# Compression weights transferred straight into the operand buffer, and a wait per attention tile in block 1's output

## The chip, the cores and the metric

The kernel runs on 1 core of one Trainium2 chip. The metric is the device time of one execution, in microseconds; lower is better. The unchanged kernel is the comparison.

## What is computed

Two transformer blocks run one after the other on 256 tokens of width 1024, all in float32. Block 1 has depth 1, block 2 has two layers. The core of it, cut to what bears on the change:

```python
def first_block(x, mem, ...):
    for l in range(DEPTH):
        x = x + 0.5 * swiglu(rms_norm(x, ffn1_norm[l]), ffn1_w_in[l], ffn1_w_out[l])
        ...
        mixed = jnp.concatenate([y_lru, y_moba.astype(x.dtype), y_mem.astype(x.dtype)], axis=-1)
        x = x + mixed @ w_out[l]
        x = x + 0.5 * swiglu(rms_norm(x, ffn2_norm[l]), ffn2_w_in[l], ffn2_w_out[l])

def compress(t, pos_emb, w1, b1, w2):
    b, s, g, d = t.shape
    chunks = t.reshape(b, s // CMP_STRIDE, CMP_STRIDE, g, d)
    blocks = jnp.concatenate([chunks[:, :-1], chunks[:, 1:]], axis=2)
    blocks = blocks + pos_emb[None, None, :, None, :]
    flat = jnp.moveaxis(blocks, 3, 2).reshape(b, -1, g, CMP_BLOCK * d)
    return jax.nn.gelu(flat @ w1 + b1) @ w2

def token_mixer(h, mem, ...):
    ...
    k_cmp = compress(kv[:, :, 0], cmp_pos_k, ck_w1, ck_b1, ck_w2)
    v_cmp = compress(kv[:, :, 1], cmp_pos_v, cv_w1, cv_b1, cv_w2)
    ...
    y_nsa = nsa_attention(q, q_rot, k_cmp, v_cmp, k_slc, v_slc, k_win, v_win, gates)
    ...
    g_conv, g_nsa, g_mem = jnp.split(jax.nn.sigmoid(merge_g), 3, axis=-1)
    merged = g_conv * (y_conv @ w_br_conv) + g_nsa * (y_nsa @ w_br_nsa) + g_mem * (y_mem @ w_br_mem)
    return merged @ w_out
```

In block 1, `mixed` has eight tiles of 128 channels: four of the recurrence (y_lru), two of the self-attention (y_moba) and two of the memory attention (y_mem). In block 2 the first matrices of `compress`, `ck_w1` and `cv_w1`, are 2048 by 256.

## The kernel before

**The weight stream.** All weights are laid out beforehand as 298 units of 128 x 2048 float32 (1 MB each) in `stream`. SyncE (`load`, line 566) brings them one after the other into `raw`, a ring of RING = 3 slots; unit n goes to slot n % 3. TensorE does a float32 product as three products of rounded parts (`product`, line 1740). So each unit is split once: ScalarE copies it to `hi`, rounded (`split_high`, line 655), and VectorE writes the rest, raw minus hi, to `lo` (`split_low`, line 1154). `hi` and `lo` are rings of three slots too.

**The counters.** `landed[s]` rises by 16 when a transfer into slot s is complete. `hi_ready`, `lo_ready` and `unit_used` rise by one for each unit, in the order of the stream: split by ScalarE, split by VectorE, last read by TensorE. `load(n)` waits until VectorE is done with unit n-3 (`lo_ready`). `split_high(n)` waits until TensorE has used unit n-3 (`unit_used`) and until unit n has landed. Each engine works through its own instructions strictly in the order written; that order is written out by hand for every engine.

**The exact units.** The four compression units of a layer (`L_EXACT`: two for the keys' `ck_w1`, two for the values' `cv_w1`) are multiplied as plain float32, not in parts. `whole` is a float32 view of the memory of `hi`. ScalarE copies such a unit from `raw` to `whole` in full precision, VectorE then writes one number to `passed` only to raise `lo_ready`, and `compressed` (line 2190) multiplies them.

**The stretch of a layer around them.** The first sixteen units after the projections are, in the order of the stream: m0, k0, k1, m1, v0, v1, m2, m3, m4 and so on, where the m are units of the merge gates, and k and v are the compression units. TensorE does m0, the scores of the first pair of attention jobs (p = 0), then k0 and k1 (`compressed(0)`), a transposition of rotated heads (rot 0), m1, rot 1, the small product hid 0, then the turn of the probabilities and the scores of pair p = 1, then v0 and v1 (`compressed(1)`), rot 2, m2, rot 3, hid 1, m3. The results go to three PSUM banks of `work` in turn. Before a result is begun, `bank_free` waits on `evac_done`, ScalarE's count of copies out of these banks: for fill f until fill f-3 has been copied. `compressed(1)` is fill 27, so it waits for the copy of m1, fill 24 (`merge_out(1)`).

ScalarE's order there (`step_work` from line 1068, called in the loop over p): exponentials of p = 0; copy of v0, copy-out of `compressed(0)`, copy-out of rot 0; copy of v1, split of m2, `merge_out(1)`, copy-out of rot 1; hid 0; copies of turned probabilities; exponentials of p = 1; split of m3; copy-out of `compressed(1)`, of rot 2; split of m4, `merge_out(2)`.

**Block 1's output.** `output` (line 2010) multiplies `mixed` by `w_out`; it begins with the four attention tiles, kt = 4 to 7 (`first=1`). `mixed_ready` says what each tile waits for; `tile_lo` counts tiles whose low part VectorE has written (`low_tile`, line 1390):

```python
                if kt == LRU_TILES:
                    pe.wait_ge(tile_lo, jobs[-1].tile)
                elif kt == KD - 1:
                    pe.wait_ge(tile_lo, jobs[-1].tile + 1)
```

`jobs[-1].tile` is 3: kt = 4 waits for three tiles, kt = 7 for all four.

Of the kernel before, what the change touches and what calls it, by code (L numbers as in the profile page):

```python
# [21 lines left out]
ACT = mybir.ActivationFunctionType  # L22
AX_X = mybir.AxisListType.X

P = 128
# [3 lines left out]
KD = D // P  # L29
D_FF = 2816  # L30
LAYERS = 2
# [25 lines left out]
RING = 3  # L57
# [10 lines left out]
B1_UNITS = B1_FFN2 + FFN_UNITS  # L68
# [6 lines left out]
L_CMP = (L_STEPS + 1, L_STEPS + 4)  # L75
L_EXACT = [n + half for n in L_CMP for half in range(2)]
# [2 lines left out]
L_FFN2 = L_OUT + 4  # L79
L_UNITS = L_FFN2 + FFN_UNITS  # L80
UNITS = B1_UNITS + LAYERS * L_UNITS


F1_MEM, F1_LRU_X, F1_QK, F1_GATE, F1_VC, F1_MEMQ, F1_FILLS = 0, 2, 4, 6, 10, 12, 15
# [54 lines left out]
class Section:  # L139
# [13 lines left out]
        return self.unit(n) % RING  # L153

    def landed(self, n):
        return 16 * (self.unit(n) // RING + 1)

    def small(self, f):
        return self.at(S1_SMALL, S_SMALL, f)
# [5 lines left out]
def wait(eng, sem, value):  # L165

    if not isinstance(value, int) or value > 0:
        eng.wait_ge(sem, value)
# [57 lines left out]
def build(nc, stream, b1_params, l_params, post_in, x_in, xT_in, mem1_in, mem1T_in, mem2_in, mem2T_in, pos_in, const_in, alibi_in, out):  # L226
    with ExitStack() as ctx:
# [12 lines left out]
        def new(name, shape, dtype=F32):  # L240
            return place(name, shape, room(4 * int(np.prod(shape[1:]))), dtype)

        raw = new("raw", [P, RING, UNIT])
        r_hi = room(4 * RING * UNIT)
        hi = place("hi", [P, RING, UNIT], r_hi, F32R)
        whole = place("whole", [P, RING, UNIT], r_hi)
# [88 lines left out]
        row_scale = new("row_scale", [P, TT])  # L335
        mem_row = new("mem_row", [P, T])
        soft = new("soft", [P, 2, 3, TT])
        passed = new("passed", [P, LAYERS * len(L_EXACT)])
        lam_t = new("lam_t", [P, 7, LRU_TILES])

        def cst(name):
# [21 lines left out]
        def sem(name):  # L363
            return ctx.enter_context(nc.semaphore(name))

        landed = [sem(f"landed{s}") for s in range(RING)]
        hi_ready, lo_ready, unit_used = sem("hi_ready"), sem("lo_ready"), sem("unit_used")
        ident_loaded, x_loaded, mem_loaded = sem("ident_loaded"), [sem(f"x_loaded{i}") for i in range(TT)], sem("mem_loaded")
        tables_loaded, half_set = sem("tables_loaded"), sem("half_set")
# [18 lines left out]
        values_done, tile_hi, tile_lo = sem("values_done"), sem("tile_hi"), sem("tile_lo")  # L388
# [124 lines left out]
        def exact(sec, n):  # L513

            return sec.layer is not None and n in L_EXACT
# [48 lines left out]
        @block.sync  # L564
        def _(sp):
            def load(n, trip=0):

                wait(sp, lo_ready, n - RING + 1 + trip * RING)
                sp.dma_start(raw[:, n % RING, :], stream[n + trip * RING]).then_inc(landed[n % RING], 16)

            def load_turns(first, end):

                with sp.Fori(0, (end - first) // RING) as trip:
                    for n in range(first, first + RING):
                        load(n, trip)

            for h in range(2):
                kts = slice(4 * h, 4 * h + 4)
                sp.dma_start(xT_raw[:, kts, :].rearrange("p k t -> p (k t)"), xT_in[:, 4 * T * h:4 * T * h + 4 * T]).then_inc(xT_loaded[h], 16)
                sp.dma_start(first_part(raw[:, 0, :], h), first_part(stream[0], h)).then_inc((first_landed, landed[0])[h], 16)  # L580
            load(1)
            for i in range(TT):
                sp.dma_start(x[:, i, :], x_in[P * i:P * i + P, :]).then_inc(x_loaded[i], 16)
            load(2)
            sp.dma_start(params[:, KD * 3:B1P_N], b1_params[:, KD * 3:B1P_N]).then_inc(params_loaded, 16)
            at = RING
            for layer in range(LAYERS):
                base = B1_UNITS + layer * L_UNITS
                turns = (base + 1 - at) // RING
                load_turns(at, at + RING * turns)  # L590
                at += RING * turns
                sp.dma_start(params[:, 0:LP_N], l_params[layer]).then_inc(params_loaded, 16)
            turns = (UNITS - at) // RING
            load_turns(at, at + RING * turns)
            for n in range(at + RING * turns, UNITS):
                load(n)
            for i in range(TT):
                for c in range(2):
                    sp.wait_ge(x_ready, 12 * (1 + LAYERS) - 3 + 2 * i + c)
                    sp.dma_start(out[P * i:P * i + P, cols(c)], x[:, i, cols(c)]).then_inc(stored, 16)  # L600
            sp.wait_ge(stored, 64)
# [53 lines left out]
        def _(act):  # L655
            def split_high(sec, n, trip=0):

                s = sec.slot(n)
                wait(act, unit_used, sec.unit(n - RING + 1) + trip * RING)
                act.wait_ge(landed[s], sec.landed(n) + trip * 16)  # L660
                dst = (whole if exact(sec, n) else hi)[:, s, :]
                nc.scalar.activation(dst, raw[:, s, :], ACT.Copy).then_inc(hi_ready, 1)  # L662

            def high_piece(sec, n, begin, end):

# [206 lines left out]
            sec = Section()  # L872
# [50 lines left out]
            for w in range(4):  # L923
                bank = by_small(sec, F1_GATE + w, S1_GATE + w)
                dst, bias = (lru_r, b1p("a_b")) if w < 2 else (lru_i, b1p("x_b"))
# [32 lines left out]
            jobs = jobs_of(sec)  # L958
# [192 lines left out]
        def _(dve):  # L1151
            step = Steps(dve, dve_step, DVE_STEPS[0], DVE_STEPS[1])

            def split_low(sec, n, trip=0):
                s = sec.slot(n)
                dve.wait_ge(hi_ready, sec.unit(n + 1) + trip * RING)
                if exact(sec, n):
                    k = len(L_EXACT) * sec.layer + L_EXACT.index(n)
                    nc.vector.memset(passed[:, k:k + 1], 0.0).then_inc(lo_ready, 1)
                    return  # L1160
                nc.vector.tensor_tensor(lo[:, s, :], raw[:, s, :], hi[:, s, :].bitcast(F32), ALU.subtract).then_inc(lo_ready, 1)  # L1161

            def low_piece(sec, n, begin, end, count):
# [575 lines left out]
        def _(pe):  # L1739
# [6 lines left out]
            def parts_ready(sec, n, trip=0):  # L1746
                pe.wait_ge(lo_ready, sec.unit(n + 1) + trip * RING)
# [396 lines left out]
            def mixed_ready(kt):  # L2144

                if kt == LRU_TILES:
                    pe.wait_ge(tile_lo, jobs[-1].tile)
                elif kt == KD - 1:
                    pe.wait_ge(tile_lo, jobs[-1].tile + 1)
                elif kt < LRU_TILES and kt % 2 == 0:  # L2150
                    pe.wait_ge(lrulo_ready, kt // 2 + 1)
# [5 lines left out]
            for layer in range(LAYERS):  # L2157
# [33 lines left out]
                def compressed(c):  # L2191

                    pe.wait_ge(cmpx_ready, layer * 2 + c + 1)
                    bank_free(sec, F_CMP[c])
                    for half in range(2):
                        n, pairs = L_CMP[c] + half, CMP_PAIRS // 2
                        parts_ready(sec, n)
                        for q in range(pairs):
                            m, g = pairs * half + q, q % STACK
                            last = nc.tensor.matmul(work[COLS * g:COLS * g + COLS, F_CMP[c] % 3, 0:CMP_HIDDEN], cmp_x[c][:, m, :],  # L2200
                                                    whole[:, sec.slot(n), CMP_HIDDEN * q:CMP_HIDDEN * (q + 1)],
                                                    start=m < STACK, stop=m >= CMP_PAIRS - STACK)
                        last.then_inc(unit_used, 1)
# [284 lines left out]
```

## Time and profile before

| | |
|---|---|
| median of 3 runs | 1747.8 us |
| lowest and highest of the runs | 1745.99 and 1747.87 us |
| the profiled execution, its own time | 1752.43 us |
| its span in the trace | 1750.5 us |
| TensorE (PE) busy | 1736.1 us, 99% of the span |
| VectorE (DVE) busy | 1073.6 us, 61% |
| ScalarE (ACT) busy | 930.8 us, 53% |
| GpSimd (POOL) busy | 34.9 us, 2% |
| moved by DMA | 328.51 MB, mean 188 GB/s |

PE is TensorE's matmuls and PEld its weight loads, which overlap them. SP is SyncE, which issues nearly all transfers. Times in the trace count from the start of the span. "Idle before" is the time in which an engine did nothing before an instruction, with what released it. Ends of matmuls are modelled, so a PE start may lie a little before the end of the row ahead of it. Layer 0 of block 2 has its compression around 765 to 778 us, layer 1 around 1401 to 1414 us, block 1 its output from 270 us on.

### The profile page before, as it was taken

The numbers are of one execution on the slowest core, as the hardware profiler recorded it, in microseconds if no ns is written. First come the engines' busy times: TensorE is split into PE (matmuls) and PEld (weight loads), VectorE is DVE, ScalarE is ACT, GpSimd is POOL, SyncE is SP. The second block draws the span as 40 slices with busy tenths as digits, with TensorE's granted clock in tenths as the row PEclk, the third lists the DMA queues.
The fourth block names the chain that finished last, engine by engine and source line by source line (L and its number), as shares of the span: only waits on it lengthen the run. The fifth ranks groups of instructions, "written<-read, shape, count | busy, mean of one in ns | idle before, by whom it ended". The sixth has DMA issues, their size and how long they took to land.

```text
span 1750.5 us, 31143 instructions
## 1 busy us (share of the span) xinstructions
PE 1736.1 (99%) x12548; PEld 1593.0 (91%) x12548; DVE 1073.6 (61%) x1502; ACT 930.8 (53%) x1271; POOL 34.9 (2%) x60
## 2 busy tenths in 40 slices
PE   9999999999999999999999999999999999999998
PEld 9999988999999999988898999899999888989997
DVE  6555787655665566546677555755584557676555
ACT  6444577444454445576756444644464587664443
POOL 0000120000000000000000000000000000000000
PEclk9999999999999999999999999999999999999999
DMA  8655434655665555553355555655554543446552
GB/s 331 235 192 190 170 121 145 219 190 193 223 227 192 190 183 194 182 200 127 139 192 181 193 192 198 231 204 195 192 204 176 191 169 121 168 158 218 190 192 96
DMA packets 47551, 328.51 MB, mean 188 GB/s; under 512 B 5488, under 2 KB 5744, under 8 KB 9072
## 3 DMA queue, kind: packets, MB, share of 16 engines
q1 hardware_dynamic: 44640, 316.86, 50.4%
q10 hardware_dynamic: 2832, 10.54, 1.6%
q8 instruction: 57, 0.93, 0.2%
q14 instruction: 22, 0.18, 0.0%
HBM read 326.33 MB, written 1.05 MB: 187 GB/s over the span
## 4 chain that ended last, share of the span: by engine, by line
PE 94%; ACT 3%; DVE 1%; issue 1%; DMA 0%; POOL 0%; SPq 0%; DVEq 0%; POOLq 0%; ACTq 0%
PE work L1742 19%; PE work L1744 19%; PE work L1743 19%; PE acc L1744 8%; PE acc L1743 8%; PE acc L1742 8%; PE work L1982 4%; PE work L1851 3%; PE acc L2066 1%; PE acc L2048 1%; ACT prob L856 1%; PE acc L2058 1%; ACT hi L662 1%; DMA xT_raw<-xT 0%; PE work L1805 0%
## 5 line engine op out<-in xcount | busy, mean ns | idle before, releaser
L1161 DVE TENSOR_TENSOR lo<-raw,hi 128x2048 fp32r<-128x2048 f32 x271 | 620.3, 2291 | 323.0 <-ACT hi L662 322.8
L662 ACT ACTIVATE hi<-raw 128x2048 fp32r<-128x2048 f32 x271 | 518.7, 1915 | 380.9 <-PE work L1744 354.0
L1742 PE MATMUL work<-xT_hi,hi 128*128 128x256 f32 x2464 | 687.5, 279 | 3.0 <-ACT merge L846 2.5
L1744 PE MATMUL work<-xT_hi,lo 128*128 128x256 f32 x2464 | 683.0, 277 | 0.0
L1743 PE MATMUL work<-xT_lo,hi 128*128 128x256 f32 x2464 | 683.0, 277 | 0.0
L1742 PEld LDWEIGHTS work<-xT_hi,hi 128*128 128x128 f32 x2464 | 463.2, 188 | 12.4 <-issue 6.9
L1743 PEld LDWEIGHTS work<-xT_lo,hi 128*128 128x128 f32 x2464 | 463.8, 188 | 2.3
L1744 PEld LDWEIGHTS work<-xT_hi,lo 128*128 128x128 f32 x2464 | 464.4, 188 | 0.0
L1744 PE MATMUL acc<-hi,hT_lo 128*128 128x512 f32 x480 | 188.8, 393 | 0.0
L1743 PE MATMUL acc<-lo,hT_hi 128*128 128x512 f32 x480 | 188.4, 392 | 0.0
L1742 PE MATMUL acc<-hi,hT_hi 128*128 128x512 f32 x480 | 186.8, 389 | 0.0
L757 ACT ACTIVATE hT_hi<-h_sb 128x512 fp32r<-128x512 f32 x55 | 34.8, 633 | 190.3 <-PE acc L1744 190.3
L1744 PEld LDWEIGHTS acc<-hi,hT_lo 128*128 128x128 f32 x480 | 90.2, 188 | 18.4
L1743 PEld LDWEIGHTS acc<-lo,hT_hi 128*128 128x128 f32 x480 | 90.1, 188 | 18.2
L1742 PEld LDWEIGHTS acc<-hi,hT_hi 128*128 128x128 f32 x480 | 90.1, 188 | 17.8
L1278 DVE TENSOR_TENSOR hT_lo<-h_sb,hT_hi 128x512 fp32r<-128x512 f32 x55 | 38.1, 693 | 100.3 <-ACT hT_hi L757 100.3
L1274 DVE TENSOR_TENSOR h_sb<-silu_a,work 128x512 f32<-128x512 f32 x61 | 41.9, 688 | 62.0 <-PE work L1744 58.9
L1266 DVE TENSOR_TENSOR silu_a<-work,norm_row 128x512 f32<-128x512 f32 x61 | 42.1, 690 | 41.6 <-PE work L1744 40.0
L856 ACT ACTIVATE prob<-prob,soft 128x256 f32<-128x256 f32 (+2 forms) x128 | 53.2, 421 | 6.4 <-DVE soft L1374 6.3
L613 POOL TENSOR_TENSOR rstd<-var,neg_half 128x1 f32<-128x1 f32 (+3 forms) x30 | 22.8, 759 | 1694.6 <-DVE var L1176 1309.0
L1742 PE MATMUL work<-br_hi,hi 128*128 128x256 f32 x176 | 49.0, 278 | 0.0
L1743 PE MATMUL work<-br_lo,hi 128*128 128x256 f32 x176 | 48.6, 276 | 0.0
(327 smaller groups left out, 2105.0 us busy)
## 6 DMA issues: line engine op xcount, KB each, us to landing
raw<-stream SPq DMA_DIRECT2D x297, 1024.0 KB, 4.8
mem_in<-mem ACTq DMA_DIRECT2D x3, 1024.0 KB, 5.0
post<-post ACTq DMA_DIRECT2D x6, 512.0 KB, 4.0
memT_raw<-mem2T ACTq DMA_DIRECT2D x2, 1024.0 KB, 7.1
xT_raw<-xT SPq DMA_DIRECT2D x2, 512.0 KB, 5.4
raw<-stream SPq DMA_DIRECT2D x2, 512.0 KB, 6.9
x<-x SPq DMA_DIRECT2D x2, 512.0 KB, 11.0
memT_raw<-mem1T ACTq DMA_DIRECT2D x1, 1024.0 KB, 11.4
```

The costliest lines, as they stand in the source:

```text
L662: nc.scalar.activation(dst, raw[:, s, :], ACT.Copy).then_inc(hi_ready, 1)
L757: nc.scalar.activation(hT_hi.rearrange("p f t -> p (f t)"), h_sb, ACT.Copy).then_inc(hThi_ready, 1)
L856: nc.scalar.activation(p, p, ACT.Exp, bias=soft[:, n % 2, 0, i:i + 1], scale=-1.0, accum_out=soft[:, n % 2, 1, i:i + 1]).then_inc(exp_read ...
L1161: nc.vector.tensor_tensor(lo[:, s, :], raw[:, s, :], hi[:, s, :].bitcast(F32), ALU.subtract).then_inc(lo_ready, 1)
L1266: nc.vector.tensor_tensor(silu_a.rearrange("p (c t) -> p c t", c=2), work[:, 0, :].rearrange("p (c t) -> p c t", c=2), norm_row.unsqueeze( ...
L1274: nc.vector.tensor_tensor(h_sb, silu_a, work[:, 1, :], ALU.mult).then_inc(h_ready, 1)
L1278: nc.vector.tensor_tensor(low.rearrange("p f t -> p (f t)"), h_sb, high.rearrange("p f t -> p (f t)").bitcast(F32), ALU.subtract).then_inc ...
L1742: nc.tensor.matmul(dst, a_hi, b_hi, start=start, stop=False)
L1743: nc.tensor.matmul(dst, a_hi, b_lo, start=False, stop=False)
L1744: return nc.tensor.matmul(dst, a_lo, b_hi, start=False, stop=stop)
L1851: last = nc.tensor.matmul(work[:, i, :], a[:, 4 * half + q, P * i:P * i + P], w[:, s, 512 * q:512 * q + 512], start=(half, turn, q) == (0, ...
L1982: last = nc.tensor.matmul(work[:, part, T * c:T * c + T], w[:, s, at:at + P], a[:, kt, :], start=(turn, c, kt) == (0, 0, 0), stop=(turn, c ...
```

## The change

Four things are edited.

- SyncE transfers the exact units straight into `whole` (`load_exact`). Since this is the memory that TensorE reads, the transfer of unit n waits for `unit_used` of unit n-3, not for `lo_ready`. Two new semaphores, `exact_landed`, count the landings, one for the first and one for the second unit of a pair. The order of issue in a layer becomes k0, m1, k1, v0, v1, m2; before it was k0, k1, m1, v0, v1, m2. SyncE's loops are cut at these places, whereby the transfer of the second layer's `params` comes behind one more unit.
- ScalarE's `split_high` does nothing for exact units: eight copies go.
- VectorE's `split_low` writes two numbers for an exact unit, to raise `hi_ready` and `lo_ready`, and waits for nothing there. TensorE waits on `exact_landed` in place of `lo_ready` in `compressed`.
- In `mixed_ready`, kt = 4 waits for two tiles, kt = 6 for three, kt = 7 for four.

```diff
--- before.py
+++ after.py
@@ -79,6 +79,7 @@
 L_FFN2 = L_OUT + 4
 L_UNITS = L_FFN2 + FFN_UNITS
 UNITS = B1_UNITS + LAYERS * L_UNITS
+EXACT_UNITS = [B1_UNITS + layer * L_UNITS + n for layer in range(LAYERS) for n in L_EXACT]
 
 
 F1_MEM, F1_LRU_X, F1_QK, F1_GATE, F1_VC, F1_MEMQ, F1_FILLS = 0, 2, 4, 6, 10, 12, 15
@@ -153,7 +154,8 @@
         return self.unit(n) % RING
 
     def landed(self, n):
-        return 16 * (self.unit(n) // RING + 1)
+        exact = sum(u <= self.unit(n) and u % RING == self.slot(n) for u in EXACT_UNITS)
+        return 16 * (self.unit(n) // RING + 1 - exact)
 
     def small(self, f):
         return self.at(S1_SMALL, S_SMALL, f)
@@ -335,7 +337,7 @@
         row_scale = new("row_scale", [P, TT])
         mem_row = new("mem_row", [P, T])
         soft = new("soft", [P, 2, 3, TT])
-        passed = new("passed", [P, LAYERS * len(L_EXACT)])
+        passed = new("passed", [P, 2 * LAYERS * len(L_EXACT)])
         lam_t = new("lam_t", [P, 7, LRU_TILES])
 
         def cst(name):
@@ -364,6 +366,7 @@
             return ctx.enter_context(nc.semaphore(name))
 
         landed = [sem(f"landed{s}") for s in range(RING)]
+        exact_landed = [sem(f"exact_landed{half}") for half in range(2)]
         hi_ready, lo_ready, unit_used = sem("hi_ready"), sem("lo_ready"), sem("unit_used")
         ident_loaded, x_loaded, mem_loaded = sem("ident_loaded"), [sem(f"x_loaded{i}") for i in range(TT)], sem("mem_loaded")
         tables_loaded, half_set = sem("tables_loaded"), sem("half_set")
@@ -570,9 +573,16 @@
 
             def load_turns(first, end):
 
-                with sp.Fori(0, (end - first) // RING) as trip:
+                turns = (end - first) // RING
+                with sp.Fori(0, turns) as trip:
                     for n in range(first, first + RING):
                         load(n, trip)
+                return first + RING * turns
+
+            def load_exact(n, half):
+
+                sp.wait_ge(unit_used, n - RING + 1)
+                sp.dma_start(whole[:, n % RING, :], stream[n]).then_inc(exact_landed[half], 16)
 
             for h in range(2):
                 kts = slice(4 * h, 4 * h + 4)
@@ -586,13 +596,20 @@
             at = RING
             for layer in range(LAYERS):
                 base = B1_UNITS + layer * L_UNITS
-                turns = (base + 1 - at) // RING
-                load_turns(at, at + RING * turns)
-                at += RING * turns
+                at = load_turns(at, base + 1)
                 sp.dma_start(params[:, 0:LP_N], l_params[layer]).then_inc(params_loaded, 16)
-            turns = (UNITS - at) // RING
-            load_turns(at, at + RING * turns)
-            for n in range(at + RING * turns, UNITS):
+                first, end = base + L_EXACT[0], base + L_EXACT[-1] + 1
+                at = load_turns(at, first)
+                for n in range(at, first):
+                    load(n)
+                load_exact(first, 0)
+                load(first + 2)
+                load_exact(first + 1, 1)
+                load_exact(first + 3, 0)
+                load_exact(first + 4, 1)
+                at = end
+            at = load_turns(at, UNITS)
+            for n in range(at, UNITS):
                 load(n)
             for i in range(TT):
                 for c in range(2):
@@ -656,10 +673,11 @@
             def split_high(sec, n, trip=0):
 
                 s = sec.slot(n)
+                if exact(sec, n):
+                    return
                 wait(act, unit_used, sec.unit(n - RING + 1) + trip * RING)
                 act.wait_ge(landed[s], sec.landed(n) + trip * 16)
-                dst = (whole if exact(sec, n) else hi)[:, s, :]
-                nc.scalar.activation(dst, raw[:, s, :], ACT.Copy).then_inc(hi_ready, 1)
+                nc.scalar.activation(hi[:, s, :], raw[:, s, :], ACT.Copy).then_inc(hi_ready, 1)
 
             def high_piece(sec, n, begin, end):
 
@@ -1153,11 +1171,12 @@
 
             def split_low(sec, n, trip=0):
                 s = sec.slot(n)
+                if exact(sec, n):
+                    k = 2 * (len(L_EXACT) * sec.layer + L_EXACT.index(n))
+                    nc.vector.memset(passed[:, k:k + 1], 0.0).then_inc(hi_ready, 1)
+                    nc.vector.memset(passed[:, k + 1:k + 2], 0.0).then_inc(lo_ready, 1)
+                    return
                 dve.wait_ge(hi_ready, sec.unit(n + 1) + trip * RING)
-                if exact(sec, n):
-                    k = len(L_EXACT) * sec.layer + L_EXACT.index(n)
-                    nc.vector.memset(passed[:, k:k + 1], 0.0).then_inc(lo_ready, 1)
-                    return
                 nc.vector.tensor_tensor(lo[:, s, :], raw[:, s, :], hi[:, s, :].bitcast(F32), ALU.subtract).then_inc(lo_ready, 1)
 
             def low_piece(sec, n, begin, end, count):
@@ -2144,6 +2163,8 @@
             def mixed_ready(kt):
 
                 if kt == LRU_TILES:
+                    pe.wait_ge(tile_lo, jobs[-1].tile - 1)
+                elif kt == KD - 2:
                     pe.wait_ge(tile_lo, jobs[-1].tile)
                 elif kt == KD - 1:
                     pe.wait_ge(tile_lo, jobs[-1].tile + 1)
@@ -2194,7 +2215,7 @@
                     bank_free(sec, F_CMP[c])
                     for half in range(2):
                         n, pairs = L_CMP[c] + half, CMP_PAIRS // 2
-                        parts_ready(sec, n)
+                        pe.wait_ge(exact_landed[half], 16 * (len(L_CMP) * layer + c + 1))
                         for q in range(pairs):
                             m, g = pairs * half + q, q % STACK
                             last = nc.tensor.matmul(work[COLS * g:COLS * g + COLS, F_CMP[c] % 3, 0:CMP_HIDDEN], cmp_x[c][:, m, :],
```

ScalarE's queue in layer 0, from the exponentials of p = 0 to the exponentials of p = 1. Before:

```order
L856 ACTIVATE prob,soft<-prob,soft 128x256 [waits scored] x4
L662 ACTIVATE whole<-raw 128x2048 [waits landed2,unit_used]
L846 ACTIVATE cmp_rows_117<-work 128x256 [waits unit_used]
L846 ACTIVATE headT<-work 128x512 [waits small_ready]
L662 ACTIVATE whole<-raw 128x2048 [waits landed0,unit_used]
L662 ACTIVATE hi<-raw 128x2048 [waits landed1,unit_used]
L846 ACTIVATE merge<-work 128x512 [waits unit_used]
L846 ACTIVATE headT<-work 128x512 [waits small_ready]
```

And in the changed kernel:

```order
L874 ACTIVATE prob,soft<-prob,soft 128x256 [waits scored] x4
L864 ACTIVATE cmp_rows_117<-work 128x256 [waits unit_used]
L864 ACTIVATE headT<-work 128x512 [waits small_ready]
L680 ACTIVATE hi<-raw 128x2048 [waits landed1,unit_used]
L864 ACTIVATE merge<-work 128x512 [waits unit_used]
L864 ACTIVATE headT<-work 128x512 [waits small_ready]
```

The two copies of v0 and v1 are gone; the split of m2 (hi<-raw) still stands right ahead of `merge_out(1)` (merge<-work), and still waits for m2's landing.

SyncE's queue in the same place. Before, all units come from one loop of three, of which this is the body:

```order
L573 UNCONDITIONAL_BRANCH
L573 ISA
L569 ISA [waits lo_ready]
L569 DMA raw<-stream 128x2048
L168 REGISTER_ALU
L569 ISA [waits lo_ready]
L569 DMA raw<-stream 128x2048
L569 ISA [waits lo_ready]
L569 DMA raw<-stream 128x2048
L573 REGISTER_ALU
L573 COMPARE_AND_BRANCH
```

In the changed kernel the loop ends two units ahead of k0, and these rows follow, with the next loop's start (its first transfer is m2):

```order
L572 DMA raw<-stream 128x2048 [waits lo_ready] x2
L585 DMA whole<-stream 128x2048 [waits unit_used]
L572 DMA raw<-stream 128x2048 [waits lo_ready]
L585 DMA whole<-stream 128x2048 [waits unit_used] x3
L577 UNCONDITIONAL_BRANCH
L577 ISA
L572 ISA [waits lo_ready]
L572 DMA raw<-stream 128x2048
```

The three transfers k1, v0 and v1 stand in a row, each behind TensorE's use of the unit three before it, and m2 stands behind v1.

## Rows read from the trace of the kernel before

**Rows 1.** The page: chain that ended last, by engine.

```profile
PE 94%; ACT 3%; DVE 1%; issue 1%; DMA 0%; POOL 0%; SPq 0%; DVEq 0%; POOLq 0%; ACTq 0%
```

**Rows 2.** Waits, PE: line waited for, us in total, times, longest us.

```profile
PE work L1742 <- ACT merge L846: 2.5, 2, 1.2
```

**Rows 3.** Timeline, PE, layer 0: start us, us, operation, [idle before <-releaser].

```profile
764.60 1.93 PE L2200 MATMUL work<-whole,cmp_x 128*32 128x256 f32 x32
...
772.89 0.60 PE L1899 MATMUL work<-const,rot 128*128 128x128 f32 x4
...
776.42 1.93 PE L2200 MATMUL work<-whole,cmp_x 128*32 128x256 f32 x32
...
785.59 0.63 PE L1899 MATMUL work<-const,rot 128*128 128x128 f32 x4 [1.19 <-ACT headT L846]
```

**Rows 4.** Timeline, ACT, layer 0.

```profile
769.59 1.90 ACT L662 ACTIVATE whole<-raw 128x2048 f32<-128x2048 f32 x1
...
772.13 1.90 ACT L662 ACTIVATE whole<-raw 128x2048 f32<-128x2048 f32 x1
773.94 1.90 ACT L662 ACTIVATE hi<-raw 128x2048 fp32r<-128x2048 f32 x1
775.73 0.58 ACT L846 ACTIVATE merge<-work 128x512 f32<-128x512 f32 x1
...
784.91 0.58 ACT L846 ACTIVATE headT<-work 128x512 f32<-128x512 f32 x1
```

**Rows 5.** Timeline, SP's DMA issues of 766 to 769 us: the transfer of m2.

```profile
767.38 0.33 SPq L569 DMA_DIRECT2D raw<-stream  x1
```

**Rows 6.** Source L569, all transfers of units: us to landing.

```profile
DMA to landing us min/median/max: 4.6/4.8/13.3
```

**Rows 7.** Windows, program start: from:to, us, four engines, clock, DMA share, GB/s.

```profile
12.00:16.00 4.00, 4.00 (x36) 3.94 (x36) 2.29 (x2) 3.38 (x6) 0.00 (x0) 1.00 1.04 431
```

**Rows 8.** DMA issues, 774 to 775 us: a transfer issued while another was in flight.

```profile
raw<-stream SPq DMA_DIRECT2D x1, 1024.0 KB, 6.0
```

**Rows 9.** DMA issues, 1403 to 1404 us: layer 1's m2, alone.

```profile
raw<-stream SPq DMA_DIRECT2D x1, 1024.0 KB, 5.8
```

**Rows 10.** Timeline, PE and ACT, layer 1.

```profile
1400.62 1.45 PEld L2200 LDWEIGHTS work<-whole,cmp_x 128*32 128x32 f32 x32 [0.33 <-issue]
...
1409.95 1.90 ACT L662 ACTIVATE hi<-raw 128x2048 fp32r<-128x2048 f32 x1
```

**Rows 11.** Windows, layer 0: same columns as rows 7.

```profile
784.00:785.00 1.00, 0.40 (x4) 0.20 (x2) 0.22 (x1) 1.00 (x3) 0.00 (x0) 1.00 0.00 0
...
788.00:789.00 1.00, 1.00 (x5) 1.00 (x6) 1.00 (x1) 0.98 (x2) 0.00 (x0) 0.50 0.76 131
```

**Rows 12.** Timeline, PE, layer 0, at the lower clock and after it.

```profile
788.20 0.41 PE L1743 MATMUL work<-xT_lo,hi 128*128 128x256 f32 x1
...
790.76 0.37 PE L1743 MATMUL work<-xT_lo,hi 128*128 128x256 f32 x1
...
791.20 0.28 PE L1743 MATMUL work<-xT_lo,hi 128*128 128x256 f32 x1
...
794.60 0.28 PE L1743 MATMUL work<-xT_lo,hi 128*128 128x256 f32 x1
```

**Rows 13.** Timeline, block 1's output: PE, then DVE.

```profile
268.41 1.08 PE L2066 MATMUL work<-probT_last,memv 128*64 128x256 f32 x8
269.90 0.47 PE L1742 MATMUL acc<-hi,mix_hi 128*128 128x512 f32 x1 [0.41 <-DVE mix_lo L1394]
...
272.05 0.39 PE L1742 MATMUL acc<-hi,mix_hi 128*128 128x512 f32 x1
...
269.34 0.42 DVE L1394 TENSOR_TENSOR mix_lo<-acc,mix_hi 128x256 fp32r<-128x256 f32 x1
271.08 0.42 DVE L1394 TENSOR_TENSOR mix_lo<-work,mix_hi 128x256 fp32r<-128x256 f32 x1 [1.33 <-ACT mix_hi L869]
```

**Rows 14.** Timeline, ACT: first use of layer 1's params.

```profile
1108.44 1.14 ACT L703 ACTIVATE xT_hi<-work,params 128x128 fp32r<-128x128 f32 x4 [2.45 <-PE work L1911]
```

## The prediction

> **What bounds the kernel now.** I read the page first. The chain that ended last is 94% TensorE and only 3% ScalarE [rows 1], so a copy taken from ScalarE is worth nothing by itself. It is worth what TensorE waits for ScalarE. The waits of TensorE show that place: 2.5 us for `merge<-work` in two waits, one in each layer [rows 2]. I then read the timeline there. A little ahead of that wait TensorE has another: it starts rot 3 after 1.19 us of idleness, released by ScalarE's copy `headT` [rows 3]. That copy starts at 784.91, and ahead of it ScalarE's rows follow each other from 769.59 on without idle time: the copy of v0, the copy of v1, the split of m2 at 773.94, `merge_out(1)` at 775.73, and so on [rows 4]. So from the split of m2 to rot 3 and m3 the stretch is bound by ScalarE. `compressed(1)` is tied to it as well: it starts at 776.42 [rows 3], 0.1 us after `merge_out(1)` ends at 775.73 + 0.58 = 776.31 [rows 4], which is its bank wait. Whatever moves the split of m2 moves TensorE by the same amount.
>
> **The change part by part.**
>
> *Copies of v0 and v1.* Two copies of 1.90 us go from ScalarE ahead of the split of m2 [rows 4]. Without them the split could start as soon as its other waits are over. One is TensorE's use of m1: the row behind m1, rot 1, starts at 772.89 [rows 3], so with 0.15 us for the end and the semaphore 773.05. That would be 773.94 - 773.05 = 0.9 us earlier in a layer. The copies of k0 and k1 stand where ScalarE is idle anyway, behind work that TensorE holds up: nothing.
>
> *The landing of m2.* This is the other wait of the split, and the change moves it. Before, m2 was issued at 767.38 [rows 5], alone, and landed after the usual 4.8 us [rows 6], at 772.2. In the changed kernel it is still issued at about 767.4, since it waits for VectorE's part of m1. But v0 and v1 are now issued right ahead of it, because they wait for TensorE's use of k0 and k1. `compressed(0)` runs from 764.60 to 766.53 [rows 3]; its first half ends near 765.6, its second at 766.5. So v0 is issued at 765.7, v1 at 766.65, m2 at 767.4: 3 MB in 1.7 us, in one queue. v0 lands at 765.7 + 4.8 = 770.5. The other two follow at the rate of a full queue. At the program's start, where transfers stand in a queue, the rate is 431 GB/s [rows 7], so 1.049 MB take 2.43 us: m2 lands at 770.5 + 4.9 = 775.4 at the earliest. From the other side, a transfer issued while another was in flight took 6.0 instead of 4.8 us [rows 8], a lag of 1.2 us: 776.6 at the latest. The split of m2 then starts at 775.4 to 776.6 instead of 773.94, +1.5 to +2.7 us. I take the early end for layer 0. In layer 1 the split started at 1409.95 and `compressed(0)` at 1400.62 [rows 10], so v0 goes at 1401.7 and m2 lands between 1411.4 and 1412.6, again +1.5 to +2.7 us. There m2 took 5.8 us even alone [rows 9], so something else delays transfers at that place, and I take the late end. Sum of both layers: **+4.2 us**, all on the path by the paragraph on the bound. What hid the transfers of v0 and v1 before was the third buffer, `raw`: they were issued before TensorE was done with k0 and k1. That cover is gone, and what is late next is m2 behind them.
>
> The Trainium skill, "DMA: Bandwidth & Descriptors", table Specifications, gives one core's share of HBM as about 358 GB/s. By it, an estimate, each megabyte would take 2.9 us, m2 would land at 776.4 in layer 0, and with the late end in both layers the sum would come to 5.4 + 1.3 - 0.4 = +6.3 us. The trace does not agree: it shows 431 GB/s, and the measurement decides.
>
> *Other waits of SyncE.* Behind k0's wait stands m1, issued about 0.5 us later than k0, still earlier than before. Behind k1 stand v0, v1 and m2, whose own waits end later. v0 and v1 land by about 774, `compressed(1)` needs them at 776.4 or later: nothing. m3 is issued behind m2, is needed some 9 us after it, and costs nothing. The params of layer 1 move behind one more unit, about 5 us later; their first use is at 1108.44 [rows 14], some 20 us after the old landing: nothing.
>
> *VectorE.* Eight more single-number writes, and the waits on ScalarE's copies are gone. `lo_ready` rises earlier for k and v, which lets m3 and m4 be issued earlier, but behind m2 in the queue: nothing.
>
> *TensorE's clock.* The new wait ahead of `compressed(1)` adds 1.5 to 2.7 us of idleness to a stretch that has already fallen to the lower level once. In 784 to 785 us TensorE was busy 0.40 us, and from 788 us its granted clock was 0.50, the 1.2 GHz level, after 1.00 before [rows 11]. At the lower level the matmuls from 788.20 to 790.76, twelve steps, came every 0.213 us; from 791.20 to 794.60, thirty steps, every 0.113 us [rows 12]. Twelve steps lose 12 x (0.213 - 0.113) = 1.2 us, and with the ends of the stretch 1.3 us. In layer 1 the same pair of waits caused no fall, so the fall is not certain. The longer wait should cause it more easily; I take one additional low stretch for the two layers together, **+1.3 us**. The bounds are -1.3 (the one that is there goes away) and +2.6 us.
>
> *Block 1's output.* TensorE's first product of it started at 269.90, after the last product of values, which began at 268.41, and it waited 0.41 us for the third tile, written at 269.34 + 0.42 = 269.76 [rows 13]. With two tiles required, its weight load can follow at 269.1, about 0.8 us earlier. kt = 6 comes two thirds of the way to kt = 7, when the third tile is there. kt = 7 began at 272.05, 2.15 us behind the first product; now it would be due at 271.3, but the fourth tile is written only at 271.08 + 0.42 = 271.50 [rows 13]. So it waits and goes at 271.65: **-0.4 us**. What is late next is that fourth tile, behind the ScalarE split that stands ahead of its high part.
>
> **The sum.** 4.2 + 1.3 - 0.4 = +5.1 us. The profiled execution took 1752.43 us, which is 4.6 us above the median of 1747.8; with the change it would take 1757.5. Added to the median, the forecast is **1752.9 us**, 0.3% slower. A measurement of this kernel can tell about 0.2%, or 3.5 us, from no change.
>
> **The rivals.**
>
> *m2 lands in time; not slower.* Place: the landing of m2. If three transfers in flight finish by 773.05, 5.65 us after m2's issue, ScalarE's chain is 0.9 us shorter in each layer and the waits of TensorE shrink by as much. The time is 1747.8 - 1.8 - 0.4 = 1745.6. For it: the usual landing takes 4.8 us, and m2 is issued when it was before. Against it: 3.1 MB between v0's first bytes, about 768, and 773 would need over 600 GB/s, and the full queue showed 431. It decides from 773.9 on: before it gain, after it loss. Chance 0.06.
>
> *Short lag and no additional low stretch.* Both layers at the early end, the clock as it was, or the present low stretch gone: 3.0 - 0.4 = +2.6 us, or +1.3 us in the latter case: 1749.1 to 1750.4. For it: 4.9 us for two megabytes is what a full queue gives. Against it: rows 8 and 9 show the lag twice. Chance 0.18.
>
> *Lag as forecast, no additional low stretch.* +3.8 us, 1751.6. For it: in layer 1 similar waits left the clock alone. Chance 0.25.
>
> *Late in both layers and a low stretch in each.* 5.4 - 0.4 + 2.6 = +7.6 us, 1755.4. For it: the wait of 2.7 us would be more than twice the longest one now, 1.2 us [rows 2], which is near where the clock fell. Chance 0.16.
>
> *The change doesn't do what it says* in block 1, because the weight load there is held by something else: +0.4 us on any case, and no case of its own.
>
> **How the numbers follow.** The forecast has 0.35, the others 0.06, 0.18, 0.25 and 0.16. The range is 1749.0 to 1756.0: it leaves out the gain and the upper part of the last case. Slower by over 0.2% (above 1751.3) are the forecast, the last case and most of the one at 1751.6: 0.35 + 0.16 + 0.20 = 0.71. Faster by over 0.2% would need 3.5 us, more than any gain above: 0.03 for what I don't see. Within 0.2%: 0.26.
>
> **What would show it.** In the changed profile ScalarE's split of m2 should have idle time before it, released by a DMA, and start near 775.5 in layer 0 and 2.7 us later than before in layer 1 (both less the 0.4 us from block 1). TensorE should show a wait of about 1.5 and 2.7 us ahead of the first product of `compressed(1)`, released by `merge<-work`, and the waits of 1.2 us should still stand behind it. A granted clock of 0.50 should follow in at least one layer. The first product of block 1's output should start near 269.1, with a short wait at kt = 7. The forecast is wrong if m2's split has no wait for a DMA, if v0, v1 and m2 land closer together than 2.4 us, or if TensorE's waits on `headT` and `merge` shrink.

## The result and the profile after

The changed kernel takes 1752.44 us (median of 11 runs, 1751.54 to 1754.15), the kernel before 1747.82 us (11 runs, 1745.99 to 1751.05). The ratio is 1.002 with a 95% interval of 1.0012 to 1.0027: the change costs between 2 and 5 us. The medians differ by 4.6 us, which lies at the upper end of that. The forecast was 1752.9.

The two profiled executions do not show this difference in their spans, 1750.5 before and 1749.9 after. The one of before was among the slowest of its kernel (1752.43), the one of after among the fastest (1751.69). `compressed(0)` of layer 0 starts at 764.60 before and 761.13 after, 3.5 us earlier, and 3.1 us of this arose between 60 and 185 us, in block 1's first feed-forward part, which the change does not touch: ScalarE's copies to `hi` start at 60.17 and 185.03 before, at 60.23 and 181.92 after. The cause of this difference between two executions stays open. So I compare stretches: from the start of `compressed(0)` to the start of m3, where the changed part lies.

The page of the changed kernel, the chain that ended last by engine (in the rows below L572 is now `load`, L680 the split, L864 the copy-outs, L2221 the compression products):

```profile
PE 94%; ACT 2%; DMA 1%; DVE 1%; issue 1%; POOL 0%; SPq 0%; DVEq 0%; POOLq 0%; ACTq 0%
```

DMA has come into the chain with 1%; before it had 0% [rows 1]. The waits of TensorE, in the form of rows 2:

```profile
PE work L2221 <- issue: 4.1, 2, 2.8
PE work L1761 <- ACT merge L864: 2.3, 2, 1.2
PE work L1918 <- ACT headT L864: 1.2, 1, 1.2
```

The first line is new: 4.1 us ahead of `compressed(1)`, once in each layer. The profile names "issue" as the releaser; the order of the rows below tells that it is `merge_out(1)`, and experiment e4 confirms it. The timeline of ScalarE, first layer 0 and then layer 1, answers to rows 4:

```profile
766.43 0.58 ACT L864 ACTIVATE headT<-work 128x512 f32<-128x512 f32 x1
772.05 1.91 ACT L680 ACTIVATE hi<-raw 128x2048 fp32r<-128x2048 f32 x1 [5.04 <-DMA raw<-stream]
773.87 0.58 ACT L864 ACTIVATE merge<-work 128x512 f32<-128x512 f32 x1
...
1409.17 1.91 ACT L680 ACTIVATE hi<-raw 128x2048 fp32r<-128x2048 f32 x1 [6.56 <-DMA raw<-stream]
```

ScalarE has lost the two copies and does nothing with the time: it waits 5.04 and 6.56 us for m2 to land. The timeline of TensorE, layer 0 and layer 1, answers to rows 3:

```profile
761.13 1.94 PE L2221 MATMUL work<-whole,cmp_x 128*32 128x256 f32 x32
...
774.54 1.93 PE L2221 MATMUL work<-whole,cmp_x 128*32 128x256 f32 x32 [1.27 <-issue]
...
783.73 0.63 PE L1918 MATMUL work<-const,rot 128*128 128x128 f32 x4 [1.20 <-ACT headT L864]
785.96 0.38 PE L1761 MATMUL work<-xT_hi,hi 128*128 128x256 f32 x1 [1.24 <-ACT merge L864]
...
1396.73 1.93 PE L2221 MATMUL work<-whole,cmp_x 128*32 128x256 f32 x32
...
1411.66 0.64 PE L2221 MATMUL work<-whole,cmp_x 128*32 128x256 f32 x8 [2.79 <-issue]
...
1423.08 0.39 PE L1761 MATMUL work<-xT_hi,hi 128*128 128x256 f32 x1 [1.03 <-ACT merge L864]
```

`merge_out(1)` ends at 773.87 + 0.58 = 774.45, `compressed(1)` starts at 774.54. Counted from the start of `compressed(0)`, the split of m2 starts at 10.9 us in layer 0 and 12.4 in layer 1; before it was 9.3 in both. m3 starts at 24.8 and 26.35; before it was 23.2 in both. That is +1.6 and +3.1 us. The old waits ahead of rot 3 and m3 still stand behind the new one in layer 0; in layer 1 only the one ahead of m3 does, and the section on the prediction tells why. m3 before, in layer 0 and layer 1:

```profile
787.82 0.58 PE L1742 MATMUL work<-xT_hi,hi 128*128 128x256 f32 x1 [1.24 <-ACT merge L846]
...
1423.84 0.38 PE L1742 MATMUL work<-xT_hi,hi 128*128 128x256 f32 x1 [1.24 <-ACT merge L846]
```

The DMA issues of v0 (762.2 to 762.5 us), v1 (763 to 763.5) and m2 (763.9 to 764.2) in layer 0, with the time to landing in the last column:

```profile
whole<-stream SPq DMA_DIRECT2D x1, 1024.0 KB, 4.8
...
whole<-stream SPq DMA_DIRECT2D x1, 1024.0 KB, 6.4
...
raw<-stream SPq DMA_DIRECT2D x1, 1024.0 KB, 8.0
```

m2 takes 8.0 us instead of 4.8 [rows 6], because two megabytes stand ahead of it.

### The profile page after: what moved, and what is told of

It is laid out like the page before. It is cut to its first block, busy times and chain, and to the rows that moved or that the text cites. A ratio compares the mean times of both kernels' runs of the same rounds, so it can differ in the third digit from the quotient of the medians.

```text
span 1749.9 us, 31085 instructions
## 1 busy us (share of the span) xinstructions
PE 1733.8 (99%) x12548; PEld 1590.6 (91%) x12548; DVE 1072.9 (61%) x1510; ACT 917.0 (52%) x1263; POOL 34.9 (2%) x60
## 4 chain that ended last, share of the span: by engine, by line
PE 94%; ACT 2%; DMA 1%; DVE 1%; issue 1%; POOL 0%; SPq 0%; DVEq 0%; POOLq 0%; ACTq 0%
PE work L1761 19%; PE work L1763 19%; PE work L1762 19%; PE acc L1763 8%; PE acc L1762 8%; PE acc L1761 8%; PE work L2001 4%; PE work L1870 3%; PE acc L2085 1%; PE acc L2067 1%; DMA raw<-stream 1%; PE acc L2077 1%; ACT hi L680 1%; ACT prob L874 1%; DMA xT_raw<-xT 0%
## 5 line engine op out<-in xcount | busy, mean ns | idle before, releaser
L680 ACT ACTIVATE hi<-raw 128x2048 fp32r<-128x2048 f32 x271 | 518.8, 1915 | 393.8 <-PE work L1763 355.0
L630 POOL TENSOR_TENSOR rstd<-var,neg_half 128x1 f32<-128x1 f32 (+3 forms) x30 | 22.8, 759 | 1694.3 <-DVE var L1195 1309.3
```

The source lines that it names most:

```text
L680: nc.scalar.activation(hi[:, s, :], raw[:, s, :], ACT.Copy).then_inc(hi_ready, 1)
```

## The experiments

Times are medians of 10 or 11 executions, of e3 only 4; the kernel before had 1748.88 us beside e1 to e4 and 1748.76 us beside e5 to e7 (27 executions each). The changed kernel was run again beside e5 to e7 only, as e7; its two medians, 1752.44 and 1752.38, agree, but beside e7 the kernel before was 0.9 us slower than in the first comparison, so differences across the groups are good to about 1 us. The last columns count from the start of `compressed(0)`, layer 0 / layer 1, in the profiled execution.

| kernel | time, us | ratio to before (95%) | split of m2 | start of m3 |
|---|---|---|---|---|
| before | 1747.82 | 1 | 9.3 / 9.3 | 23.2 / 23.2 |
| changed | 1752.44 | 1.0012 to 1.0027 | 10.9 / 12.4 | 24.8 / 26.35 |
| e1 tiles only | 1747.95 | 0.9992 to 1.0010 | 9.3 / 9.3 | 23.2 / 23.2 |
| e2 m2 between v0 and v1 | 1748.76 | 0.9986 to 1.0004 | 9.4 / 10.0 | 23.4 / 23.9 |
| e3 one more megabyte | 1757.28 | 1.0030 to 1.0061 | 14.9 / 14.7 | 28.8 / 28.6 |
| e4 merge_out first | 1751.94 | 1.0011 to 1.0029 | 11.5 / 12.1 | 24.9 / 25.5 |
| e5 m2 ahead of both | 1746.16 | 0.9975 to 0.9993 | 8.7 / 8.9 | 22.7 / 22.8 |
| e6 keys direct only | 1749.05 | 0.9992 to 1.0010 | 9.4 / 9.4 | 23.3 / 23.3 |
| e7 changed again | 1752.38 | 1.0016 to 1.0034 | 11.0 / 12.2 | 24.9 / 26.1 |

**The waits per tile alone** (e1), in the kernel before:

```diff
                 if kt == LRU_TILES:
+                    pe.wait_ge(tile_lo, jobs[-1].tile - 1)
+                elif kt == KD - 2:
                     pe.wait_ge(tile_lo, jobs[-1].tile)
```

> The kernel before, with the new waits per attention tile in block 1's output and nothing else. My account: about -0.4 us against the kernel before (1747.4), the first product of the output starts near TensorE's last product of values with a short wait at the fourth tile. Rival (the wait is held by something else): +-0 us, and the first product starts where it did.

The time does not tell it from no change, as 0.4 us lies inside the interval. The timeline of TensorE does:

```profile
264.60 1.08 PE L2066 MATMUL work<-probT_last,memv 128*64 128x256 f32 x8
265.61 0.50 PE L1742 MATMUL acc<-hi,mix_hi 128*128 128x512 f32 x1
...
267.55 0.40 PE L1744 MATMUL acc<-hi,mix_lo 128*128 128x512 f32 x1
267.79 0.46 PE L1742 MATMUL acc<-hi,mix_hi 128*128 128x512 f32 x1
268.08 0.39 PE L1743 MATMUL acc<-lo,mix_hi 128*128 128x512 f32 x1
```

The first product starts 1.01 us after the last products of values begin; before it was 269.90 - 268.41 = 1.49 us [rows 13]. kt = 7 starts 3.19 us after them, before 272.05 - 268.41 = 3.64. It is hardly held up (a step of 0.29 instead of 0.23 us behind it), and 0.36 us are left of the gain at the end. So the gain is there and is small; in the time it was not resolved.

**m2 between v0 and v1** (e2), in the changed kernel:

```diff
                 load_exact(first + 3, 0)
+                load(end)
                 load_exact(first + 4, 1)
-                at = end
+                at = end + 1
```

> The changed kernel with one edit: SyncE issues m2 between v0 and v1 instead of behind both. All transfers into the operand buffer and all missing copies stay. Landing theory (the loss is m2 landing behind v0 and v1): m2 lands near 773.0 on the clock of the trace before, ScalarE's split of it starts 0.8 us earlier than in the kernel before, and the time falls below both kernels, to about 1745.8. Rival (the loss comes with the direct transfers themselves, their landing or their writes into the memory that TensorE reads): it stays near 1752.

Measured: 1748.76 us, between the two. The loss is gone, and so the rival is out: every direct transfer and every missing copy is still there. But nothing is gained. The split of m2, layer 0 and layer 1:

```profile
770.15 1.91 ACT L681 ACTIVATE hi<-raw 128x2048 fp32r<-128x2048 f32 x1 [3.56 <-DMA raw<-stream]
...
1405.48 1.91 ACT L681 ACTIVATE hi<-raw 128x2048 fp32r<-128x2048 f32 x1 [4.12 <-DMA raw<-stream]
```

With `compressed(0)` at 760.71 and 1395.48 these are 9.4 and 10.0 us, not the 8.5 expected. I had given the second transfer in the queue 2.4 us behind the first; it landed 3.1 and 3.8 us behind it.

**One more megabyte ahead of m2** (e3), in the changed kernel. `spare` is a new semaphore; SyncE waits for it only ahead of m4, which goes into the same slot of `raw`:

```diff
                 load_exact(first + 4, 1)
-                at = end
+                sp.dma_start(raw[:, (end - 1) % RING, :], stream[end - 1]).then_inc(spare, 16)
+                load(end)
+                load(end + 1)
+                sp.wait_ge(spare, 16 * (layer + 1))
+                load(end + 2)
+                at = end + 3
```

> The changed kernel with one more megabyte transferred (v1 once more, into a slot of raw that nothing reads then) ahead of m2 in each layer. Landing theory: each split of m2 starts 2.4 us later, together +4.9 us against the changed kernel, 1757.3. Rival (the number of transfers ahead of m2 does not matter): no difference from the changed kernel, 1752.4.

Measured: 1757.28 us, 4.8 us above the changed kernel. The expectation was 4.9; that it agrees to a tenth is luck, as the 95% interval of the ratio is over 5 us wide. One megabyte more per layer on SyncE's queue, which nobody reads, costs 4.8 us in the two layers together. Split of m2 and TensorE's wait, layer 0:

```profile
775.87 1.91 ACT L685 ACTIVATE hi<-raw 128x2048 fp32r<-128x2048 f32 x1 [9.02 <-DMA raw<-stream]
...
778.37 3.64 PE L2226 MATMUL work<-whole,cmp_x 128*32 128x256 f32 x32 [5.45 <-issue]
```

In the single execution the two layers moved by 4.0 and 2.2 us, not 2.4 each; a lag, told of below, fell into both here and into one of them in the changed kernel.

**merge_out(1) ahead of the split of m2** (e4), in ScalarE's order of the changed kernel:

```diff
                     if kind == "merge":
+                        if k == 1:
+                            merge_out(k)
                         split_high(sec, L_MERGE[k] + 2)
                         if k < 2:
                             split_high(sec, L_CMP[k] + 2)
-                        merge_out(k)
+                        if k != 1:
+                            merge_out(k)
```

> The changed kernel with ScalarE's merge_out(1) ahead of the split of m2. Landing theory: TensorE's wait ahead of compressed(1) is gone, but ScalarE's chain up to rot 3 and m3 is shortened only by the 0.6 us of that copy in each layer, so the waits move to m2, rot 3 and m3: about -1.2 us against the changed kernel, 1751.2. Rival (what costs is the bank wait of compressed(1) alone): -4.2 us, 1748.2.

The bank wait of `compressed(1)` is gone and 4 us are not. Layer 0, the rows with idle time behind the start of `compressed(1)`, which comes at 772.65:

```profile
774.80 0.63 PE L1921 MATMUL work<-const,rot 128*128 128x128 f32 x4 [0.22 <-ACT headT L864]
776.65 0.36 PE L1764 MATMUL work<-xT_hi,hi 128*128 128x256 f32 x1 [1.21 <-DVE lo L1183]
783.45 0.63 PE L1921 MATMUL work<-const,rot 128*128 128x128 f32 x4 [0.91 <-ACT headT L864]
785.68 0.38 PE L1764 MATMUL work<-xT_hi,hi 128*128 128x256 f32 x1 [1.24 <-ACT merge L864]
```

The wait has moved to rot 2 and to m2, which now waits for VectorE's part of m2. The rival (the bank wait alone costs) is out. The gain of 0.5 us is smaller than the 1.2 expected, and the measurement does not resolve it. From the split of m2 to m3 the chain is 0.5 us shorter in each layer, but in layer 0 m2 landed 0.6 us later than in the changed kernel.

**m2 ahead of both** (e5), in the changed kernel:

```diff
+                load(end)
                 load_exact(first + 3, 0)
                 load_exact(first + 4, 1)
-                at = end
+                at = end + 1
```

> The changed kernel with m2 issued ahead of v0 and v1. Landing theory: m2 lands 4.8 us after its issue again (near 7.6 us after the start of compressed(0)), so ScalarE's split of it waits only for TensorE's use of m1 and starts near 8.5 us after the start of compressed(0), against 9.3 in the kernel before and 10.9 to 12.4 in the changed one. v1 lands at 12.5 to 14 and may hold compressed(1) up to 1 us, which the wait ahead of rot 3 takes in. The time: 0.8 us in each layer and 0.4 us in block 1 below the kernel before, about -2.0 us; against the changed kernel about -6. Rival (writes of v0 and v1 into the memory that TensorE reads, or their late landing, are what costs): not below the kernel before.

This beats both kernels: 1746.16 us, 2.6 us below the kernel before beside it (1.2 to 4.4 by the interval), 6.2 below the changed one. The split in layer 0 and layer 1, then TensorE in layer 0:

```profile
770.10 1.91 ACT L681 ACTIVATE hi<-raw 128x2048 fp32r<-128x2048 f32 x1 [2.85 <-PE work L1764]
...
1403.92 1.91 ACT L681 ACTIVATE hi<-raw 128x2048 fp32r<-128x2048 f32 x1 [3.00 <-DMA raw<-stream]
...
775.23 1.07 PE L2222 MATMUL work<-whole,cmp_x 128*32 128x256 f32 x16 [0.73 <-DMA whole<-stream]
...
784.02 0.39 PE L1762 MATMUL work<-xT_hi,hi 128*128 128x256 f32 x1 [0.86 <-ACT merge L865]
```

In layer 0 the split now waits for TensorE (its use of m1) and no longer for a DMA. In layer 1 m2 lagged, and the split still waits for it, but starts only 0.14 us later than in layer 0. v1 lands late and holds the second half of `compressed(1)` for 0.73 us, and there is no wait left ahead of rot 3. m3 starts 0.55 and 0.4 us earlier than in the kernel before. With block 1's 0.4 us that is 1.4 us; the rest of the 2.6 us may be the clock, told of below, and was not tried by itself.

**Only the keys direct** (e6): `EXACT_UNITS` holds the first two of each layer, v0 and v1 are loaded, copied and waited for as before; the core of the edit:

```diff
-                if exact(sec, n):
+                if exact(sec, n) and n in L_EXACT[:2]:
                     return
...
-                load_exact(first + 3, 0)
-                load_exact(first + 4, 1)
-                at = end
+                at = first + 3
```

> Half of the change: only k0 and k1 go straight into the operand buffer, v0 and v1 go through raw and ScalarE's copies as before; the waits per attention tile are in. Landing theory: nothing stands ahead of m2 in the queue, its split starts 9.3 us after the start of compressed(0) as before, and the time is that of the kernel before less 0.4 us. Rival (direct transfers cost in themselves): half of the loss stays, about +2 us against the kernel before.

The time is that of the kernel before, and the split of m2 is at 9.4 us in both layers. The rival is out: its +2 us lies beyond the interval (at most +1.7), and m3 starts at 23.3 in both layers, where before it was 23.2. The direct transfers of the keys cost nothing in themselves; of those of the values e5 shows it. The 0.4 us are again below what the measurement resolves.

**The changed kernel again** (e7):

> The changed kernel once more, unedited, beside the others on the same chip: +4 to +5 us against the kernel before. The split of m2 again 1.5 us late in a layer where m2 follows v1 without a lag, 2.7 to 3.1 us where there is one. Which of its layers shows a stretch at the lower clock is not fixed; on the account that a low stretch between compressed(1) and rot 3 is taken in by the wait ahead of rot 3, such a stretch moves the start of m3 by less than 0.3 us.

The difference from the kernel before beside it is 3.6 us, below the 4 to 5 expected. The places are as expected: the split of m2 is 1.7 and 2.8 us late, the lag falls into the same layer as in the first profile, and the stretch at the lower clock in layer 1 does not move m3.

## Why the prediction was right, step by step

**The bound.** Right. TensorE followed the split of m2 one for one: in the changed kernel +1.6 and +3.1 us at the split, the same at m3, and in e3, e2 and e5 m3 moves with it in both directions, in e5 less, as v1 takes over.

**The landing of m2.** Forecast +1.5 us in layer 0 and +2.7 in layer 1, measured +1.6 and +3.1. e2, e3 and e5 settle the cause: with the same transfers and the same copies missing, the order of SyncE's queue alone moves the time from 1752.4 (m2 last) over 1748.8 (in the middle) to 1746.2 (first), and one more megabyte ahead of m2 moves it to 1757.3. v0 landed after 4.8 us, and in a full queue m2 followed v1 by 2.49 us in layer 0, which is 421 GB/s; I had taken 2.43. The Trainium skill, "DMA: Bandwidth & Descriptors", table Specifications, puts the ceiling on the way into SBUF at 435 GB/s beside its 358 GB/s for HBM. The measured rate lies just below the first and well above the second.

**The lag.** I took it for layer 1 from one row [rows 9] without knowing what it is. In the changed kernel it was 1.4 us, between v0 and v1. Where v1 or m2 lagged by more than 1 us, one packet of the instruction queue stands in the trace at that time. In the changed kernel, DMA from 1403 to 1405 us, the lagging layer:

```profile
q1 hardware_dynamic: 113, 0.80, 96.8%
q8 instruction: 1, 0.02, 2.8%
```

From 763 to 771 us, while v1 and m2 of layer 0 moved, there is none:

```profile
q1 hardware_dynamic: 400, 3.01, 94.9%
```

In e5 the packet of layer 0 came at 772.9 and v1, then on its way, landed 3.8 us behind v0; in layer 1 it came at 1398.7 and m2 took 6.1 us. The two rows on which the prediction's late end rests have it too: in the kernel before a packet came at 776.04, in the flight of the transfer of rows 8, and at 1404.37, in that of rows 9. So the 6.0 us of rows 8 were no price of another transfer in flight, as I had read them; in the changed kernel queued transfers without a packet land 2.5 us apart.

But the packet does not explain every lag. In e2, layer 0, m2 landed 3.1 us behind v0, 0.6 us more than 2.5, and from 762 to 772 us the instruction queue moved nothing:

```profile
q1 hardware_dynamic: 457, 3.36, 88.9%
```

In e4, layer 0, v1 lagged by 0.5 us, also without one. Nor does every packet cost time: in the kernel before one came at 759.29, near the end of a transfer that was issued at 754.85, and that one took the usual 4.8 us. This is a coincidence seen in traces, not an experiment, and what the small lags are stays open.

**TensorE's clock.** This term, +1.3 us, was mis-sized, and it is the step that failed. The additional low stretch did come, in layer 1, as the windows of the changed kernel show (granted clock in the column before DMA share):

```profile
1411.00:1412.00 1.00, 0.34 (x8) 0.31 (x12) 0.89 (x1) 1.00 (x3) 0.00 (x0) 1.00 0.85 352
1413.00:1414.00 1.00, 1.00 (x12) 0.27 (x4) 1.00 (x5) 0.99 (x4) 0.00 (x0) 0.50 0.04 16
1414.00:1416.00 2.00, 2.00 (x13) 1.80 (x10) 0.79 (x7) 1.98 (x3) 0.00 (x0) 0.50 0.66 197
1417.00:1420.00 3.00, 3.00 (x29) 3.00 (x28) 1.57 (x6) 3.00 (x8) 0.00 (x0) 1.00 0.22 90
```

But it cost nothing. From `compressed(1)` to m3 it is 785.96 - 774.54 = 11.42 us in layer 0 at the full clock, and 1423.08 - 1411.66 = 11.42 us in layer 1 with the low stretch inside, so here it moved m3 by nothing. ScalarE's chain runs in parallel there and sets rot 3 and m3; the wait ahead of rot 3 took in the slower matmuls. e7 shows it again (11.42 and 11.43 us), and e3 with a longer one: in layer 0 the clock was low for 6 us,

```profile
776.00:782.00 6.00, 3.63 (x33) 1.64 (x33) 3.69 (x11) 5.95 (x9) 0.00 (x0) 0.51 0.56 202
```

and from the split of m2 to m3 it was 28.8 - 14.9 = 13.9 us, as in the changed kernel (24.8 - 10.9). A low stretch behind m3, as in the kernel before [rows 11, 12], does cost time. The next copy of a merge result on ScalarE, in the kernel before, layer 0 and layer 1:

```profile
795.04 0.60 ACT L846 ACTIVATE merge<-work 128x512 f32<-128x512 f32 x1 [3.21 <-PE work L1744]
...
1429.61 0.60 ACT L846 ACTIVATE merge<-work 128x512 f32<-128x512 f32 x1 [1.76 <-PE work L1744]
```

It starts 795.04 - 787.82 = 7.22 us behind m3 with the low stretch and 1429.61 - 1423.84 = 5.77 us without it: 1.45 us. In the other profiles it is 5.8 to 6.0 us without such a stretch, and 7.3 to 7.5 with one (layer 1 of e2 and e4, both layers of e6). Neither profile of the changed kernel had one there. In these two executions the term was 0 in place of +1.3, and -1.45 against the profile of before, whose low stretch is gone. That is why the two profiled spans do not show the loss: 3.5 us less up to `compressed(0)`, 1.6 and 3.1 more in the layers, 1.45 less behind m3 make -0.2 us in sum, the spans differ by -0.6.

What the term is in the median, no profile shows. Of the changed kernel's first eleven executions, five with a mean granted clock of 0.997 took 1753.0 to 1754.2 us, and six with 0.998 or 0.999 took 1751.5 to 1752.4; the profiled one, 1751.7, is of the second kind. The kernel before has both kinds too: beside e5, three executions at 0.997 took 1751.4 to 1752.9 us, seven at 1.000 took 1746.6 to 1748.9. So here the executions at the lower mean clock are the slower ones, in either kernel, though in e7 the groups overlap; where in the program they lose the time is not shown.

e5, which has less idle time of TensorE here, had no low stretch in its profile before the last microseconds and the narrowest spread of all, 1745.4 to 1747.0 us in 11 runs against 1746.6 to 1752.9 for the kernel before. In its executions the mean granted clock was 0.999 or 1.000. Among those at 1.000 e5 has a median of 1746.4 us and the kernel before 1748.1, a difference of 1.7 us, close to the 1.4 us of the stretches. That the clock makes up the rest of the 2.6 us fits this, but was not tried by itself.

**Block 1's output.** -0.4 forecast, -0.36 in the trace of e1. The working was off in its parts: the first product came 0.5 us earlier, not 0.8, and so kt = 7 hardly waited.

**The other terms.** Other waits of SyncE, VectorE's writes and the later params showed no wait, as forecast. The sum by stretches is 1.6 + 3.1 - 0.4 = +4.3 us; the medians differ by 4.6 and 3.6. The forecast of +5.1 had a lag too small by 0.5 us in the two layers and a clock term too large by 1.3, so that the errors partly cancel. That the time came out within 0.5 us of the forecast is in part luck: the kernel before moved by 0.9 us between the comparisons.

## What to carry to other kernels

A copy through a staging buffer can be what lets a transfer start early: when it is dropped, the transfer waits for the reader of the final buffer, and everything behind it in the queue comes later, even if it waits for nothing itself. So ask not only when the direct transfers land, but which unit behind them is due first, and issue that one ahead of them. Here the order of three lines on an idle engine decided between 4 us lost (3.6 and 4.6 in two comparisons) and 2.6 us gained.

## What the runs showed of the hardware

Three megabytes issued within 1.7 us from one queue land one after the other: in the changed kernel v0 after 4.8 us as if it were alone, v1 2.5 us (layer 0) or 3.9 us (layer 1) behind it, m2 another 2.5 us behind. The lags of 1.1 to 1.4 us of v1 and m2 all fell together with a single packet of 16 KB of the instruction queue; smaller lags of 0.5 and 0.6 us also came without one. And a stretch at the lower clock right behind a long wait of TensorE cost nothing where ScalarE's chain set the next start (11.42 us with and without it), and 1.45 us where it came behind m3.
